# A tuned two-block transformer kernel: half of two feed-forward blocks is computed token tile by token tile, under the norm of the other tile

## The reference

```python
h = h + rmsnorm(merged @ w_out[l], norm_mix_post[l])      # 1024 -> 1024

n2 = rmsnorm(h, norm_ffn_pre[l])
gu = n2 @ w_ffn_in[l]                                     # 1024 -> 2 x 2816
ff = (jax.nn.silu(gu[..., :D_FF]) * gu[..., D_FF:]) @ w_ffn_out[l]
h = h + rmsnorm(ff, norm_ffn_post[l])
```

## Time and profile before

| | |
|---|---|
| median of 3 runs | 1171.9 us (1170.99 to 1172.2) |
| the profiled execution | 1170.55 us |
| its span, first to last instruction | 1168.7 us |
| TensorE busy | 1058.4 us, 91% |
| VectorE busy | 811.7 us, 69% |
| ScalarE busy | 390.0 us, 33% |
| mean granted TensorE clock | 0.996 of 2.4 GHz |

### The profile page before, as it was taken

The page is one execution under the profiler, slowest core; times in us unless marked ns, Lnnn a source line. Parts: engine busy times, 40 slices in busy tenths (PEclk is TensorE's granted clock), DMA queues, the critical chain, the costliest instruction groups (busy, mean ns, idle before and its releaser), DMA issues.

```text
span 1168.7 us, 12638 instructions
## 1 busy us (share of the span) xinstructions
PE 1058.4 (91%) x4468; PEld 688.2 (59%) x4468; DVE 811.7 (69%) x1704; ACT 390.0 (33%) x724; POOL 268.9 (23%) x261
## 2 busy tenths in 40 slices
PE   8999899998998878899877777889999999999998
PEld 7888464454354333344322222269887878999986
DVE  5787988777777767787887776765555576555543
ACT  6673312211221111321111012045765445444532
POOL 0002445434444334344333343400000000000000
PEclk9999999999999999999999999999999999999999
DMA  9848999999999999999999999976434534555540
GB/s 349 336 164 299 422 421 422 421 420 421 419 420 421 422 422 421 421 413 417 417 420 421 406 420 410 412 272 239 144 144 144 180 145 163 181 183 182 183 174 36
DMA packets 55535, 371.91 MB, mean 318 GB/s; under 512 B 6192, under 2 KB 7345, under 8 KB 12081
## 3 DMA queue, kind: packets, MB, share of 16 engines
q0 software_dynamic: 36864, 268.45, 55.5%
q1 hardware_dynamic: 18608, 102.65, 23.8%
HBM read 370.03 MB, written 1.05 MB: 318 GB/s over the span
## 4 chain that ended last, share of the span: by engine, by line
PE 54%; DMA 32%; DVE 9%; issue 3%; ACT 1%; POOL 1%; DVEq 0%; SPq 0%; POOLq 0%; ACTq 0%
DMA uv<-in_peer_uv,eidx 31%; PE bank L1823 12%; PE bank L1825 11%; PE bank L1824 11%; PE bank L2124 11%; DVE uv L1516 4%; PE bank L1895 3%; PE bank L1794 1%; DVE diag L1530 1%; POOL uv L700 1%; DVE xn L1693 0%; DVE tmp L1686 0%; PE bank L1967 0%; PE bank L1934 0%; DMA wraw<-in_in_vb 0%
## 5 line engine op out<-in xcount | busy, mean ns | idle before, releaser
L2124 PE MATMUL bank<-uv,diag 128*128 128x512 f32 x1024 | 489.6, 607 | 95.6 <-DVE diag L1530 94.4
L1516 DVE SCALAR_TENSOR_TENSOR uv<-uv,xn 128x1024 f32<-128x1024 f32 x256 | 313.6, 1225 | 141.1 <-DMA uv<-in_peer_uv,eidx 139.4
L2124 PEld LDWEIGHTS bank<-uv,diag 128*128 128x128 f32 x1024 | 179.3, 190 | 370.1 <-issue 367.7
L700 POOL DMA_INDIRECT uv<-in_peer_uv,eidx x256 | 268.6, 1049 | 481.7 <-PE bank L2124 360.4
L1233 DVE TENSOR_TENSOR w_lo<-wraw,w_hi 128x2048 fp32r<-128x2048 f32 x71 | 162.3, 2290 | 118.8 <-ACT w_hi L776 118.8
L987 ACT ACTIVATE chosen<-chosen 128x1 f32<-128x1 f32 x256 | 51.8, 203 | 511.8 <-DVE uv L1516 511.5
L776 ACT CAST w_hi<-wraw 128x2048 fp32r<-128x2048 f32 x71 | 135.1, 1906 | 65.4 <-PE bank L1825 65.3
L1823 PE MATMUL bank<-nT_hi,w_hi 128*128 128x256 f32 x432 | 122.4, 283 | 0.8 <-DVE nT_lo L1254 0.8
L1824 PE MATMUL bank<-nT_lo,w_hi 128*128 128x256 f32 x432 | 122.3, 283 | 0.0
L1825 PE MATMUL bank<-nT_hi,w_lo 128*128 128x256 f32 x432 | 122.3, 283 | 0.0
L1530 DVE TENSOR_SCALAR diag<-const,chosen 128x128 f32<-128x128 f32 x256 | 89.2, 348 | 4.9 <-ACT chosen L987 4.8
(11 more groups left out here) (271 smaller groups left out, 1190.1 us busy)
## 6 DMA issues: line engine op xcount, KB each, us to landing
wraw<-in_ff_in SPq DMA_DIRECT2D x22, 1024.0 KB, 4.8
wraw<-in_ff_out SPq DMA_DIRECT2D x11, 1024.0 KB, 4.7
wraw<-in_query SPq DMA_DIRECT2D x4, 1024.0 KB, 5.5
uv<-in_peer_uv,eidx POOLq DMA_INDIRECT x256, 13.4
wraw<-in_in_q SPq DMA_DIRECT2D x2, 1024.0 KB, 10.1
wraw<-in_in_k SPq DMA_DIRECT2D x2, 1024.0 KB, 10.3
wraw<-in_pool_o SPq DMA_DIRECT2D x2, 1024.0 KB, 4.7
wraw<-in_sb_o SPq DMA_DIRECT2D x2, 1024.0 KB, 4.7
```

Source lines behind the costliest of these rows:

```text
L700: pool.indirect_dma_start(out=uv[:, RING_AT[n % RING], :], out_offset=None, in_=io["peer_uv"], in_offset=bass.IndirectOffsetOnAxis(ap=eidx ...
L1516: nc.vector.scalar_tensor_tensor(out=u, in0=u, scalar=1.0, in1=xn[:, head // PEER_HEADS, :], op0=ALU.mult, op1=ALU.mult, accum_out=hdot[he ...
L2124: mm = nc.tensor.matmul(acc[m][:, :], diag[:, n % RING, :], uv[:, RING_AT[n % RING], D + m * HALF:D + (m + 1) * HALF], start=(n % (ROWS // ...
```

## The change

The first two blocks of the feed-forward, `ff_in0` and `ff_in1`, are computed token tile by token tile, with the normed values stationary and the weight moving, so that tokens lie on the partitions. Tile 0's part of both blocks (48 products) stands where `keep_warm` stood, ahead of the transposes of tile 1; tile 1's part follows them. One bank `ff_t` per tile holds both blocks. The products of gate and other half (`h32`, 256 channels of 128 tokens) are turned by two transposes per tile (`turn_h`), tile 0's ahead of `ff_in2` and tile 1's ahead of `ff_in3`, into a bank `hT`, and rounded from there. The split parts of `ff_in0` and `ff_in1` get places of their own (`w_hi_first`, `w_hi_ff1` and their low parts), and both engines split these blocks earlier.

```diff
+SLOT_OF |= {f"ff_in{j}": "out2_1b" for j in (2, 3, 4)}
...
+        w_hi_ff1 = place("w_hi_ff1", 54 * KB, [P, WB], F32R)
+        w_lo_ff1 = place("w_lo_ff1", 62 * KB, [P, WB], F32R)
...
# ScalarE, norms of w_out2
                     half_square(src[:, :], 4, t, m)
+                    if (t, m) == (0, 0):
+                        act.wait_ge(merged_ready, 2 * NT)
+                        split_to("ff_in1")
                     if (t, m) == (1, 0):
-                        split_to("ff_in0")
                         for h in range(2):
                             round_tile("n2T", nT_hi, 0, h)
...
# ScalarE, feed-forward
-                if j < FC:
+                if j < 2:
+                    src = wait_full(act, "ff_t", j)
+                    nc.scalar.activation(two(silu[:, j, :]), by_half(src)[:, :, 0, :], ACT.Silu).then_inc(silu_ready, 1)
+                elif j < FC:
                     src = wait_full(act, "ff", j)
-                    if j >= 2:
-                        wait_read(act, "ff", j - 2)
+                    wait_read(act, *(("ff_t" if j < 4 else "ff"), j - 2))
                     nc.scalar.activation(silu[:, j % 2, :], src[:, 0:S], ACT.Silu).then_inc(silu_ready, 1)
-                if j >= 1:
+                if j in (1, 2):
+                    src = wait_full(act, "hT", j - 1)
+                    nc.scalar.copy(hT_hi[:, 0:2, tok(j - 1)], two(src[:, 0:S])).then_inc(product_rounded, 1)
+                elif j > 2:
...
# VectorE, norms of w_out2
                     gain_half(4, t, m, lambda m: ("w_out2", m, t))
+                    if (t, m) == (0, 0):
+                        split_to("ff_in0")
                     if (t, m) == (1, 0):
-                        split_to("ff_in0")
+                        split_to("ff_in1")
...
# VectorE, feed-forward
+                if j in (1, 2):
+                    dve.wait_ge(product_rounded, j)
+                    t = j - 1
+                    nc.vector.tensor_tensor(hT_lo[:, 0:2, tok(t)], two(bank[at("hT", t)[0]][:, 0:S]),
+                                            hT_hi[:, 0:2, tok(t)].bitcast(F32), ALU.subtract).then_inc(read_of("hT", t), 1)
...
# TensorE
-            keep_warm(22, "n2T", 1, 0)
+            def ff_tokens(t):
+
+                for j in range(2):
+                    w = split_block(f"ff_in{j}")
+                    dst = bank[at("ff_t", t)[0]] if j else open_bank("ff_t", t)
+                    for c in range(KC):
+                        if j == 0 and c % (KC // 2) == 0:
+                            wait_read(pe, "n2T", t, c // (KC // 2))
+                        mm = product(dst[:, j * S:(j + 1) * S], parts(nT, ALL, c, tok(t)),
+                                     parts(w, ALL, slice(c * S, (c + 1) * S)), start=(c == 0), stop=(c == KC - 1))
+                mm.then_inc(full_of("ff_t", t), 1)
+
+            def turn_h(t):
+
+                wait_read(pe, "ff_t", t)
+                transposes(h32[:, t, :], "hT", t)
+
+            ff_tokens(0)
             turn_n2(1)
-            for j in range(FC):
-                channels_out(f"ff_in{j}", nT, "ff", j, turned="n2T" if j == 0 else None)
+            ff_tokens(1)
+            for j in range(2, FC):
+                if j < 4:
+                    turn_h(j - 2)
+                channels_out(f"ff_in{j}", nT, "ff", j)
+            for t in range(NT):
+                wait_read(pe, "hT", t)
```

More of the change, by code:

```diff
@@ L85, in last_product @@
         return (name[4:5] + "2", int(part))
+    if name in ("ff_in0", "ff_in1"):
+        return ("ff_t", NT - 1)
     if name.startswith("ff_in"):
@@ L249, in psum_uses @@
             use("w_out2", n, t)
-    both("n2T")
-    for j in range(FC):
+    for t in range(NT):
+        for h in range(2):
+            use("n2T", t, h)
+        use("ff_t", t)
+    for j in range(2, FC):
+        use("hT", j - 2) if j < 4 else None
         use("ff", j)
@@ L522, in four, with by_half @@
             return ap.rearrange("p (c k) -> p c k", c=4)
+        def by_half(ap):
+            return ap[:, :].rearrange("p (j a k) -> p j a k", j=2, a=2)
         def two(ap):
@@ L555, in split_slot @@
                 return w_hi_out2[:, :], w_lo_out2[:, :]
+            if name == "ff_in0":
+                return w_hi_first[:, :], w_lo_first[:, :]
+            if name == "ff_in1":
+                return w_hi_ff1[:, :], w_lo_ff1[:, :]
             if name == "in2_va":
@@ L767, in split_to @@
                     raw = wait_loaded(act, SPLIT[s])
-                    if s >= S_SLOTS and SPLIT[s] not in ("out0b", "in2_va", "out2_1b"):
+                    if s >= S_SLOTS and SPLIT[s] not in ("out0b", "in2_va", "out2_1b", "ff_in0", "ff_in1"):
                         done = last_product(SLOT_OF[SPLIT[s]])
@@ L1757, in _ @@
             for j in range(FC + 1):
-                if j < FC:
+                if j < 2:
                     dve.wait_ge(silu_ready, j + 1)
-                    if j >= 2:
-                        dve.wait_ge(ffT_ready, j - 1)
+                    src = bank[at("ff_t", j)[0]]
+                    nc.vector.tensor_tensor(two(h32[:, j, :]), two(silu[:, j, :]), by_half(src)[:, :, 1, :],
+                                            ALU.mult).then_inc(read_of("ff_t", j), 1)
+                elif j < FC:
+                    dve.wait_ge(silu_ready, j + 1)
+                    if j < 4:
+                        wait_full(dve, "hT", j - 2)
+                    else:
+                        dve.wait_ge(ffT_ready, j - 3)
                     src = bank[at("ff", j)[0]]
@@ L2285, in _ @@
                             turn_n2(0)
-            keep_warm(22, "n2T", 1, 0)
-            turn_n2(1)
-            for j in range(FC):
-                channels_out(f"ff_in{j}", nT, "ff", j, turned="n2T" if j == 0 else None)
+            def ff_tokens(t):
[12 more added lines that the diff above has]
+            ff_tokens(0)
+            turn_n2(1)
+            ff_tokens(1)
+            for j in range(2, FC):
+                if j < 4:
+                    turn_h(j - 2)
+                channels_out(f"ff_in{j}", nT, "ff", j)
+            for t in range(NT):
+                wait_read(pe, "hT", t)
             for j in range(FC // 2):
-                pe.wait_ge(ffT_ready, 2 * j + 2)
+                if j:
+                    pe.wait_ge(ffT_ready, 2 * j)
                 rows_out(f"ff_out{j}", (hT_hi, hT_lo), j == 0, j == FC // 2 - 1, 2 * j, lambda t, n: ("ff_out", t, n))
```

## The result

| | before | changed |
|---|---|---|
| median, us | 1171.45 (1170.91 to 1172.2, 4 runs) | 1164.45 (1163.75 to 1166.03, 4 runs) |
| profiled execution, us | 1170.55 | 1164.26 |
| its span, us | 1168.7 | 1162.4 |
| granted clock | 0.996 | 0.994 |

The ratio is 0.9945 (95% interval 0.9929 to 0.996), 4.7 to 8.3 us faster. The forecast was 1166.7, in a range of 1165.2 to 1168.6: the direction was right, and the time lies 0.75 us under the range.

The account below looks back on a forecast made before the run. TensorE, busy 91%, was taken as the bound, with one hole under tile 1's norm. Moved products -5.76 us and turns +0.56 gave -5.20: 1165.35 from the profiled execution, 1166.7 by the median, range 1165.2 to 1168.6.

Parts of the forecast that it names:

- The hole: On TensorE between out2_1b and ff_in0, 968.40 to 976.41: 8.01 us whose only useful work is eight transposes.
- the products of 0.120 us with the roles swapped: In ff_in0 and ff_in1, a 256-column product with values stationary still costs 0.120 us; 48 moved ahead give -5.76 us.
- the transposes where they were: Tile 1's transposes still start when xn releases them at 974.27, or 0.05 us late if the first product costs 0.08.
- the unmoved 0.83 us wait: TensorE's wait for nT_lo behind tile 1's transposes; that chain stays where it is and products resume at 976.41.
- the free splits with 1.1 us of margin: Earlier splits on ScalarE and VectorE cost 0; tile 0's rests end at 967.25, TensorE asks at 968.40.
- The local sum: Around the feed-forward's start: -5.76 us for the moved products plus 0.56 for the turns, -5.20 us.
- the two turns of h: turn_h(0) and turn_h(1), two new transposes each on TensorE: 0.28 us a turn, 0.56 both, bounds 0.20 to 0.87.
- the last one of the sum: Whole kernel: from the profiled execution's 1165.35 to the runs' median, 1.35 us higher, giving 1166.7.
- A: At the turns of h: they or their waits cost more, 0.87 us a turn, gain 4.02, time 1167.9; 7%.
- B: Under tile 1's norm: tile 0's products are held up 5 us by their inputs, no change, 1171.9; 4%.
- C: In ff_in0 and ff_in1: the swapped form is as slow as 512 columns, 0.230 us a product, 1177.2; 2%.
- D: Around tile 1's transposes: the clock falls without the filler; 15 us at 1.2 GHz would give 1174.2; 1%.

Follow-up runs that it names:

- the room half filled: The changed kernel with 11 filler products put ahead of tile 0's 48 products: median 1166.12 us, ratio 0.9966 to the kernel before.

## Why the prediction was wrong

**The mechanism held in each step.** The hole, its content, the products of 0.120 us with the roles swapped, the transposes where they were, the unmoved 0.83 us wait, the free splits with 1.1 us of margin, the weight queue (no wait of TensorE for a weight in the stretch): all as forecast. In one place the prediction's own sum slips: with 0.08 for a first product tile 0's share would have ended at 968.40 + 5.76 + 0.08 = 974.24, 0.03 ahead of the transposes and not 0.05 late. Measured, that first product costs nothing extra (0.11 to the next), and the 48 leave 0.12 us of room. The local sum was -5.20, and the stretch gave -5.33. The term that was a little off is *the two turns of h*: 0.28 each by the price of eight transposes, 0.22 measured, since a pair right ahead of products takes 0.13 and not 0.20. That is 0.12 of the 0.13.

**The step that failed is the last one of the sum, with its range:** "the median of the runs is 1.35 higher, 1171.9, and by it the forecast is 1166.7", and from it a low end of 1165.2. I took a median of three executions as the kernel's level and let the range follow it with about a microsecond for the spread. The 29 executions of the kernel before in the first set of experiments go from 1168.15 to 1171.64 with a median of 1169.20, the next sets have 1169.64 and 1169.48: the three of the prediction, 1170.99 to 1172.2, lay at the top or above. The four of the changed kernel, median 1164.45, lie only 0.6 to 0.8 over what it showed later (1163.88 and 1163.65). So of the 7.0 us between the medians of the first comparison 5.3 are the edit, and the rest is that the kernel before stood high. The later differences of medians, with more executions of the kernel before, are 5.3 and 5.8 us. With their level the same sum comes out: 1169.20 - 5.20 = 1164.0, and 1163.88 was measured beside it. Why the first four stood so high stays open. Of the 65 executions of the kernel before that came later, on three chips, 6 reached 1170.91; all four of the first comparison did, which four draws from the 65 would hardly give. The chip of the first comparison is not on record, so another chip or its state at that hour is a rival to chance that nothing here tests.

By the sum against the profiled execution, which the prediction also gives (1165.35), less the 0.13 and the 0.98 us ahead of the stretch, it is 1164.24, the profiled execution of the changed kernel to 0.02. This is bookkeeping with the measured parts, not a forecast: the 0.98 us were luck, and without them that execution would have lain near 1165.2, at the low end of the range.

What the trace of before could have told: its chain runs through the gathers and the load of in2_vb for some 30% of the span, so its end depends on DMA landings; a range around a small local gain has to carry that. Two us on either side of the sum's own range (1166.3 to 1167.9), the size of the 2.3 us that the starts spread over, would have held the 1164.45; two on either side of 1166.7 would not.

**The rivals.** A (turns of 0.87) and B (the hole not filled) are refuted by the turns done twice and by the stretch. C (slow swapped form) is refuted: 24 products from 967.42 to 970.29. D did not occur, and the kernel without the filler shows that its mechanism is real: 2.9 us for an empty hole. The changed kernel's hole holds work, and its clock stays at 1.00. The Trainium skill ("TensorE: Matmul & The Clock Gate", Part 4: PE-mode transpose) states that a transpose does not count as a busy TensorE in the same way as a product. The 0.50 under the eight transposes without the filler does not speak against it, but no run here separates them from the idleness ahead. The 275 ns that the prediction takes from the same part of the Trainium skill stand there for a bf16 transpose; the float32 ones here last 0.27 us each, and in a pair each costs 0.11.

**Open.** In twelve profiles that share those instructions in2_vb's second piece keeps ScalarE waiting for nothing (the room half filled) up to 2.18 us (the kernel before, again). Why it varies was not tried, nor why the kernel before stood high in the first comparison.

## What to carry to other kernels

Fill the wait under a reduction with products that need only the other tile, even if that means computing a block in the other orientation: a change of form costs only the turns, here 0.22 us for a pair. Work placed there is free up to the length of the chain above it and costs what goes beyond (2.27 us for 2.37 us of filler in a full room), so measure the room first and check what supplies it; and a filler that keeps the clock up must be replaced, not just dropped. For a local change, judge by the distance between two events around it in the trace, which repeats to 0.01 us here. Take the level of the total time from more than three executions, and give it a range that holds the spread of DMA waits elsewhere.

## What the runs showed of the hardware

- A 256-column product at 1.2 GHz takes 0.213 us start to start and 0.120 at 2.4 GHz: less than double, so expecting 0.24 was wrong.
- 5.71 us of idleness were enough for the clock to be at 1.2 GHz under the instructions that followed, and it was back at 2.4 GHz only near 981.5, after 2 us of transposes and some 5.6 us of dense products.
- Two 128x128 float32 transposes ahead of products take 0.13 us, and the product behind them is followed 0.09 later than others; two ahead of two more take 0.22.
- The changed kernel, profiled three times, reaches the stretch at times 1.08 us apart (966.34 to 967.42), and twelve profiles with the same instructions up to there spread over 2.31 us, all of it ahead of 772 us.
